# Attention mixers of a two-block kernel: head norms of the keys by tokens, the gates' remainders on another engine, three merge buffers, two weight loads placed anew

## The chip, the cores and the metric

The kernel runs on one core of one Trainium2 chip. The metric is the device time of one execution in microseconds (us). Engines are named PE (TensorE, matmuls), PEld (its weight loads), DVE (VectorE), ACT (ScalarE), POOL (GpSimd) and SP (SyncE, which here issues the DMAs).

## The reference, cut to what matters

The program is two transformer-like blocks in float32 on 256 tokens of width 1024. The first has two layers, each an FFN, a *mixer* and an FFN; then come an even mixer, an MLP, an odd mixer and an MLP. The change touches only the two mixers (stages m0 and m1) of the first block.

```python
h = rms_norm(x, mix_norm[l])
(nq, nkc, nvc, nks, nvs, nkw, nvw, ngate, sq, sk, sv, wq, wk, wv, bgate) = jnp.split(h @ w_in[l], ...)
y_nsa = nsa_attention(...)   # 8 query heads, 2 key heads: compressed, selected and window keys
y_sb = stick_breaking_attention(...)           # 4 heads, sq, sk, sv
y_swa = swa_sink_attention(...)                # 4 query heads, 2 key heads, wq, wk, wv
g = sigmoid(bgate).reshape(B, S, 3, 1024)
merged = g[:, :, 0] * (y_nsa @ w_up_nsa[l]) + g[:, :, 1] * (y_sb @ w_up_sb[l]) + g[:, :, 2] * (y_swa @ w_up_swa[l])
x = x + merged @ w_out[l]
```

Inside the attentions, queries and keys of each head (64 values) are normed: `rms_norm(q, q_norm)`, `rms_norm(k, k_norm)`. The compressed keys and values are `silu(blocks @ w1) @ w2`, the compressed key is normed too.

## The kernel before, in words

Activations lie with features on the 128 partitions and the 256 tokens along the free side. A float32 product is made of three matmuls on rounded halves (`product`, L675 to L677): the weights and the activations are split into a rounded part and a remainder. Every weight block is a **unit** of up to 128x2048 words, streamed through three raw buffers and three split buffers (AHEAD = 3). For a unit, SP loads the raw words, ACT copies the rounded part (`hi`, L1579, two halves), DVE or POOL subtracts to get the remainder (`lo`, DVE L2326, POOL L3302, two halves), and PE multiplies. A raw buffer is loaded again when the remainder of its unit is written (for kind "raw", when PE is done with it); a rounded part may be written when PE is done with the unit three places before. SP issues all loads in the order of the list made in `plan_mixer`. Each engine runs its own program in order; a call `hi(U[...] + 3)` stands where the engine prepares the unit three places further in the list.

A mixer runs, on PE: projections of the stick-breaking q, k, v; then queries and keys of the others, interleaved with `stick(0)` to `stick(5)` (stick-breaking attention) and `compress(kv, half)` (the w1 products, 32 matmuls of 30 columns each); `all_values` (values and head gates); then 24 *gates* (`gate(n)`, 24 matmuls of 256 columns each, for the 12 units "bg"), which are spread between the ten attention jobs of the list `jobs` (2 of kind "w", 8 of kind "n"): for job i, `second(i)` (transposes of P), `scores(i+1)`, `gate(4+2i)`, `third(i)` (times V), `gate(5+2i)`. Last are the three products "up" for each of 8 output blocks o, merged on DVE and POOL with the gates, and the product with w_out ("wo").

Head norms. For queries, `querysum` makes the mean squares with tokens on the partitions (8 numbers for a token), `querymean` copies them, and one root and one reciprocal with a Newton step (`exact`) serves all 24 columns; the factors are applied to the scores. For the keys "nk" (512 columns) and "wk" (256), `headsum` makes the means spread over all 128 partitions, `headroot` (ACT) takes the root, and `headnorm` (DVE: `exact`, five instructions on the whole width, L2603 to L2616, then a multiplication, L2629) scales the key. On PE, `third` waits for values, on DVE `first(x)` makes the biased scores and their maximum (L2536 or L2539, L2545), ACT the exponential (L1769), and `then(x)` the normed P (L2562 to L2573). `least` and `gated` do the same for the compressed keys; `compressed(1)` on PE transposes their result. PSUM banks go round in a ring of seven.

The remainders of the units three places after "bg" 1 to 11 are made by POOL, all others in the mixer by DVE. The merging uses two buffers `b.tm`.

The mark that PE awaits before the first "up" product:

```python
for x in new(at(s, "attended", "dve")):
    pe.wait_ge(*x)
```

Of the kernel before, what the change touches and what calls it, by code (L numbers as in the profile page):

```python
# [213 lines left out]
class Map:  # L214
# [158 lines left out]
    def lay_mixer(self):  # L373
# [15 lines left out]
        b.ms, b.rq = take(24), take(24)  # L389
# [17 lines left out]
        b.tm = [grid(take(768), c=3) for _ in range(2)]  # L407
# [145 lines left out]
    def plan_mixer(self, l):  # L553
# [29 lines left out]
        self.unit((s, "w2"), [(0, 128, kv * 128, 128, 2, 0, 64, t[f"nsa_cmp_{n}_w2"][l].rearrange("(k p) n -> p k n", p=128))  # L583
                              for kv, n in ((0, "k"), (1, "v"))], 256, "raw", 64)
        for blk in range(1, 12):
            gate(blk)
# [52 lines left out]
HN = {("q", 0): 0, ("q", 1): 1, "nk": 0, ("q", 2): 1, "wk": 0, "kc": 1}  # L639

# [10 lines left out]
def tensor_program(pe, L, M):  # L651
# [210 lines left out]
    def mixer(s, was, l):  # L862
# [27 lines left out]
        def querysum(name):  # L890
# [3 lines left out]
            for c in range(4):  # L894
                ins = pe.matmul(b[:, 2 * c:2 * c + 2], b_.hn[HN[name]][:, c * 128:c * 128 + 128], M.blk64[:, 0:128:64],
                                start=True, stop=True)
            ins.then_inc(*done((s, name, "ms"), (s, name, "hn")))

# [71 lines left out]
        querysum(("q", 0))  # L970
# [10 lines left out]
        querysum(("q", 1))  # L981
# [6 lines left out]
        headsum("nk", 512)  # L988
# [5 lines left out]
        querysum(("q", 2))  # L994
# [15 lines left out]
        headsum("wk", 256)  # L1010
        compress(1, 0)
        all_values(1)
        compress(1, 1)
# [9 lines left out]
        m = U[s, "w2"]  # L1023
        v2 = M.raw(m).rearrange("p (k n) -> p k n", k=4)
        b = bank(s, "kc")
        ready(m)
        for x in new(at(s, "hidT", 0, "s")):
# [10 lines left out]
        ins.then_inc(*done((s, "vc"), ("unit", m)))  # L1038
        gate(1)
# [527 lines left out]
def scalar_program(act, L, M):  # L1567
# [217 lines left out]
    def mixer(s, was, l):  # L1785
# [82 lines left out]
        headroot("nk", 512)  # L1868
# [8 lines left out]
        headroot("wk", 256)  # L1877
        for x in new(*[at(s, ("q", i), "msv") for i in range(3)]):
# [10 lines left out]
        hi(U[s, "va", 1] + 3)  # L1889
        hidden(1)  # L1890
        hi(U[s, "w1", 1, 1] + 3)
# [17 lines left out]

        gate(0)  # L1910
        headsq("kc", M.bank(s, "kc")[:, 0:15], 15, ("kc",))
        hi(U[s, "w2"] + 3)
# [4 lines left out]
        gate(1)  # L1917
# [20 lines left out]
        gate(2)  # L1938
        headroot("kc", 15)
        weights(0)  # L1940
# [23 lines left out]
        for blk in range(4):  # L1964
            for j in range(2):
# [5 lines left out]
                act.activation(b_.Mr[:, o, :], b_.tm[o % 2][:, 0, :], ACT.Copy, scale=1.0).then_inc(*done((s, "Mh", o)))  # L1971
# [316 lines left out]
def vector_program(dve, L, M):  # L2288
# [286 lines left out]
    def mixer(s, was, l):  # L2575
# [55 lines left out]
        def querymean(x_):  # L2631
            name = ("q", x_)
# [988 lines left out]
```

## Time and profile before

| | before |
|---|---|
| median of 3 runs | 2646.88 us (2639.64 to 2652.54) |
| the profiled execution, its own time | 2644.85 us |
| its span in the trace | 2642.9 us (1.95 us lie around it) |
| PE busy | 2514.2 us, 95% |
| DVE, ACT, POOL busy | 1628.0, 1189.7, 470.0 us |
| mean granted clock of PE | 0.970 of full speed |
| mixer m0 | about 240 to 503 us of the span |
| mixer m1 | about 940 to 1202 us |

The span is what the profiler saw from the first to the last instruction. A granted clock of 1.00 is 2.4 GHz, of 0.50 it is 1.2 GHz; PE has no other level here, and a number between is a mean over a stretch. A matmul counts as busy also where it runs at half the clock.

### The profile page before, as it was taken

Reading aid. Unit: us, or ns where it says so; the run is one execution under the profiler, and the core shown is the slowest. Engines: PE = TensorE matmul, PEld = TensorE weight load, DVE = VectorE, ACT = ScalarE, POOL = GpSimd, SP = SyncE. Lnnn points to the kernel's source line nnn. Section 1 sums busy time; section 2 is a strip of 40 time slices with the busy share of each in tenths; the row PEclk is TensorE's granted clock in tenths of the full one; section 3 lists DMA queues with packets and bytes.
Section 4 is the critical chain, followed back from the end, with each engine's and each line's share of the span. In section 5 each row is a group of like instructions: output and inputs, shape, how many; then the busy total and the mean of one; then the engine's idle time right before and its main releaser. Section 6 shows DMA issues by size and latency. Waiting matters only on the chain.

```text
span 2642.9 us, 42197 instructions
## 1 busy us (share of the span) xinstructions
PE 2514.2 (95%) x17977; PEld 2333.5 (88%) x17977; DVE 1628.0 (62%) x2410; ACT 1189.7 (45%) x1952; POOL 470.0 (18%) x429
## 2 busy tenths in 40 slices
PE   8999979999999898899999988999999999999998
PEld 7999879999999898799998764888888999999998
DVE  4777656677888865657776676553343654556753
ACT  5444446544444454455544444342232443444653
POOL 1321015432022100362423120200001011001000
PEclk8999879999999998899999998999999999999999
DMA  6667444476766755346777220132323333334563
GB/s 220 213 213 219 122 144 112 150 233 214 249 222 227 236 149 169 93 125 220 255 259 219 64 76 1 48 112 96 94 98 92 126 96 98 110 105 135 165 197 101
DMA packets 386384, 401.65 MB, mean 152 GB/s; under 512 B 44695, under 2 KB 370611, under 8 KB 385940
## 3 DMA queue, kind: packets, MB, share of 16 engines
q1 hardware_dynamic: 383448, 391.19, 47.3%
q10 hardware_dynamic: 2748, 7.76, 0.8%
q8 instruction: 141, 2.31, 0.4%
q14 instruction: 47, 0.39, 0.0%
HBM read 394.72 MB, written 4.19 MB: 151 GB/s over the span
## 4 chain that ended last, share of the span: by engine, by line
PE 73%; DVE 17%; ACT 6%; issue 2%; DMA 2%; POOL 1%; ACTq 0%; DVEq 0%; SPq 0%; POOLq 0%
PE bank L675 22%; PE bank L676 21%; PE bank L677 21%; DVE rounded L2326 5%; DVE plain L2315 3%; ACT rounded L1579 3%; PE bank L683 2%; PE bank L688 2%; PE bank L1515 1%; DVE plain L2573 1%; POOL plain L3366 1%; PE bank L1078 1%; DMA plain<-in_w_in 1%; PE bank L1108 0%; DVE plain L2562 0%
## 5 line engine op out<-in xcount | busy, mean ns | idle before, releaser
L675 PE MATMUL bank<-rounded 128*128 128x256 f32 (+1 forms) x3704 | 1126.2, 304 | 24.8 <-DVE rounded L2326 9.7
L676 PE MATMUL bank<-rounded 128*128 128x256 f32 (+1 forms) x3704 | 1107.3, 299 | 0.0
L677 PE MATMUL bank<-rounded 128*128 128x256 f32 (+1 forms) x3704 | 1106.3, 299 | 0.0
L2326 DVE TENSOR_TENSOR rounded<-plain,rounded 128x1024 fp32r<-128x1024 f32 (+2 forms) x574 | 671.3, 1216 | 486.5 <-ACT rounded L1579 486.2
L675 PEld LDWEIGHTS bank<-rounded 128*128 128x128 f32 x3704 | 721.8, 195 | 60.8 <-DVE rounded L2326 12.5
L1579 ACT ACTIVATE rounded<-plain 128x1024 fp32r<-128x1024 f32 (+1 forms) x630 | 616.9, 1032 | 341.5 <-PE bank L677 283.9
L676 PEld LDWEIGHTS bank<-rounded 128*128 128x128 f32 x3704 | 722.6, 195 | 16.6
L677 PEld LDWEIGHTS bank<-rounded 128*128 128x128 f32 x3704 | 722.0, 195 | 16.6
L675 PE MATMUL bank<-rounded,rounded 128*128 128x256 f32 (+2 forms) x1472 | 453.9, 308 | 24.0 <-DVE rounded L2326 18.4
L676 PE MATMUL bank<-rounded,rounded 128*128 128x256 f32 (+2 forms) x1472 | 451.1, 306 | 0.0
L677 PE MATMUL bank<-rounded,rounded 128*128 128x256 f32 (+2 forms) x1472 | 449.6, 305 | 0.0
L675 PEld LDWEIGHTS bank<-rounded,rounded 128*128 128x128 f32 x1472 | 280.4, 190 | 41.3 <-DVE rounded L2326 21.6
L676 PEld LDWEIGHTS bank<-rounded,rounded 128*128 128x128 f32 x1472 | 282.9, 192 | 12.4
L677 PEld LDWEIGHTS bank<-rounded,rounded 128*128 128x128 f32 x1472 | 281.5, 191 | 11.6
L3302 POOL TENSOR_TENSOR rounded<-plain,rounded 128x1024 fp32r<-128x1024 f32 x56 | 133.6, 2409 | 449.5 <-ACT rounded L1579 449.5
L2315 DVE SCALAR_TENSOR_TENSOR plain<-plain 128x1024 f32<-128x1024 f32 x140 | 189.8, 1402 | 1.4 <-DMA plain<-in_ada_w 0.8
L3366 POOL TENSOR_TENSOR plain<-plain 128x256 f32<-128x256 f32 x88 | 72.6, 832 | 402.7 <-ACT plain L1739 391.4
L1739 ACT ACTIVATE plain<-plain 128x256 f32<-128x256 f32 x88 | 36.9, 419 | 195.7 <-DVE plain L2501 195.7
L688 PE MATMUL bank<-plain 128*128 128x128 f32 (+2 forms) x475 | 73.6, 297 | 53.3 <-DVE plain L2573 20.5
L3319 POOL TENSOR_TENSOR plain<-plain 128x256 f32<-128x256 f32 (+1 forms) x64 | 58.4, 913 | 358.9 <-ACT plain L1633 356.8
L688 PEld LDWEIGHTS bank<-plain 128*128 128x128 f32 (+2 forms) x475 | 56.8, 147 | 65.2 <-DVE plain L2573 20.2
L683 PE MATMUL bank<-plain 128*128 128x30 f32 (+5 forms) x564 | 101.6, 337 | 2.2 <-POOL plain L3429 2.0
(302 smaller groups left out, 2090.7 us busy)
## 6 DMA issues: line engine op xcount, KB each, us to landing
plain<-in_mlp_w SPq DMA_DIRECT2D x64, 1024.0 KB, 5.3
plain<-in_ada_w SPq DMA_DIRECT2D x48, 1024.0 KB, 5.4
plain<-in_ffn_w_gate SPq DMA_DIRECT2D x44, 1024.0 KB, 5.5
plain<-in_ffn_w_up SPq DMA_DIRECT2D x44, 1024.0 KB, 5.9
plain<-in_ffn_w_down SPq DMA_DIRECT2D x32, 1024.0 KB, 5.2
plain<-in_w_in SPq DMA_DIRECT2D x32, 1024.0 KB, 5.3
plain<-in_od_w_in SPq DMA_DIRECT2D x32, 1024.0 KB, 5.7
plain<-in_ffn_w_down SPq DMA_DIRECT2D x16, 768.0 KB, 5.4
```

The lines of the kernel that those rows point to most:

```text
L675: pe.matmul(dst, a[0], b[0], start=first and i == 0, stop=False)
L676: pe.matmul(dst, a[0], b[1], start=False, stop=False)
L677: ins = pe.matmul(dst, a[1], b[0], start=False, stop=last and i == n - 1)
L683: ins = pe.matmul(dst, a, b, start=first and i == 0, stop=last and i == n - 1)
L688: ins = pe.transpose(o, i, ident[0:i.shape[0], 0:i.shape[0]])
L1579: act.activation(top, raw, ACT.Copy, scale=1.0).then_inc(*done(("hi", m, half)))
L1739: act.activation(f.sg[:, c % 4, :], f.sg[:, c % 4, :], ACT.Silu, bias=0.0, scale=1.0).then_inc(*done((s, "silu", c)))
L2315: dve.scalar_tensor_tensor(acc, raw[:, i, :], M.cc[:, k, v:v + 1], acc, MUL, ADD).then_inc(*done(*keys))
L2326: dve.tensor_tensor(low, raw, top, SUB).then_inc(*done(("lo", m, half)))
L3302: pool.tensor_tensor(low, raw, top, SUB).then_inc(*done(("lo", m, half)))
L3319: pool.tensor_tensor(acc, acc, sq[c % 2], ADD).then_inc(*done((s, "acc", c)))
L3366: pool.tensor_tensor(f.sg[:, c % 4, :], f.sg[:, c % 4, :], f.up[c % 4], MUL).then_inc(*done((s, "gu", c)))
```

## The change

1. Keys "nk" and "wk" get their mean squares by tokens too (`tokensum`, `tokenmean`), beside the queries: `b.ms` and `b.rq` grow from 24 to 36 columns, and one root and one `exact` serve all. As the keys need their factor along the free side and on all partitions of a head, PE then spreads it (`keyfactors`: 12 matmuls of 128 columns with a broadcast column as weights) into two banks, and DVE multiplies (`keyscale`).
2. All remainders of the gates' units go to DVE: three ahead of and beside the first job, one at the end of each job i (`lo(U[s, "bg", 2 + i] + 3)`). POOL has none left in a mixer.
3. Merging goes round in three buffers, and POOL makes the remainder of block o-1 after the sums of block o.
4. w2 is no unit any more: SP loads it into its own 256 words by two DMAs of 64 KB, beside the third unit after the first query block. The second half of w1 for the values stands behind gate unit 0 in the list, and `compress(1, 1)` behind `gate(0)` on PE. `hidden(1)` and the splits on ACT are placed to match.

```diff
@@ plan_mixer
         values(1)
-        w1(1, 1)
-        def gate(blk):
+        for blk in range(12):
+            if blk == 1:
+                w1(1, 1)
             self.square((s, "bg", blk), w, 0, 8, 2584 + blk * 256, 256)
-        gate(0)
-        self.unit((s, "w2"), [...], 256, "raw", 64)
-        for blk in range(1, 12):
-            gate(blk)
@@ tensor_program
+MS = {("q", 0): 0, ("q", 1): 8, ("q", 2): 16, "nk": 24, "wk": 32}
-        def querysum(name):
+        def tokensum(name, n=4):
...
+        def keyfactors():
+            for x in new(at(s, "rq")):
+                pe.wait_ge(*x)
+            for name, n in (("nk", 4), ("wk", 2)):
+                b = bank(s, name, "r")
+                for c in range(n):
+                    for g in range(2):
+                        f = MS[name] + 2 * c + g
+                        ins = pe.matmul(b[g * 64:g * 64 + 64, c * 128:c * 128 + 128], b_.rq[:, f:f + 1].to_broadcast([128, 64]),
+                                        ident, start=True, stop=True)
+                ins.then_inc(*done((s, name, "r")))
-        headsum("nk", 512)
+        tokensum("nk")
         stick(4)
...
         all_values(0)
-        headsum("wk", 256)
+        tokensum("wk", 2)
         compress(1, 0)
         all_values(1)
-        compress(1, 1)
...
         gate(0)
-        m = U[s, "w2"]
+        compress(1, 1)
+        keyfactors()
+        gate(1)
         (products "kc" and "vc" with w2)
-        gate(1)
@@ scalar_program
-        headroot("nk", 512)
         hi(U[s, "wq"] + 3)
...
         hi(U[s, "va", 0] + 3)
-        headroot("wk", 256)
-        for x in new(*[at(s, ("q", i), "msv") for i in range(3)]):
+        for x in new(*[at(s, name, "msv") for name in MS]):
             act.wait_ge(*x)
         act.activation(b_.rq, b_.ms, ACT.Sqrt, ...)
         hidden(0)
         hi(U[s, "w1", 1, 0] + 3)
-        hi(U[s, "va", 1] + 3)
-        hidden(1)
-        hi(U[s, "w1", 1, 1] + 3)
         (evictions of the values, the head gates)
+        hi(U[s, "va", 1] + 3)
         gate(0)
+        hidden(1)
+        gate(1)
         headsq("kc", ...)
-        hi(U[s, "w2"] + 3)
         (eviction of "vc")
-        gate(1)
         gate(2)
+        weights(0)
         headroot("kc", 15)
-        weights(0)
+        hi(U[s, "w1", 1, 1] + 3)
         gate(3)
@@ vector_program
+        def keyscale(name, dst, n):
+            for x in new(at(s, name, "r"), L.last()):
+                dve.wait_ge(*x)
+            dve.tensor_tensor(dst, dst, M.bank(s, name, "r")[:, 0:n], MUL).then_inc(*done((s, name, "s"), ("free", s, name, "r")))
         headscale(("q", 2), ...)
-        headnorm("nk", b_.nk, 512)
+        tokenmean("nk")
         lo(U[s, "wq"] + 3)
...
         stick(5)
+        tokenmean("wk", 4)
         lo(U[s, "va", 0] + 3)
-        headnorm("wk", b_.wk, 256)
-        exact((s, "rqroot"), b_.rq, b_.ms, b_.cst[:, 0:24])
+        exact((s, "rqroot"), b_.rq, b_.ms, b_.hnt[:, 0:36])
         lo(U[s, "w1", 1, 0] + 3)
         lo(U[s, "va", 1] + 3)
         hidden(1)
-        lo(U[s, "w1", 1, 1] + 3)
-        lo(U[s, "bg", 0] + 3)
+        keyscale("nk", b_.nk, 512)
+        keyscale("wk", b_.wk, 256)
         headscale("kc", ...)
-        lo(U[s, "w2"] + 3)
         first(0)
+        lo(U[s, "bg", 0] + 3)
+        then(0)
         headnorm("kc", b_.kc[:, 0:15], 15)
-        then(0)
+        lo(U[s, "w1", 1, 1] + 3)
+        lo(U[s, "bg", 1] + 3)
         for i in range(n):
             (first(i + 1), then(i + 1), least or gated, keep of job i)
+            lo(U[s, "bg", 2 + i] + 3)
         here(s, "attended", "dve")
-                b, b2, tm = M.bank(s, "up", o), M.bank(s, "up2", o), b_.tm[o % 2]
-                for x in new(..., at(s, "M", o - 2) if o >= 2 else None):
+                b, b2, tm = M.bank(s, "up", o), M.bank(s, "up2", o), b_.tm[o % 3]
+                for x in new(..., at(s, "M", o - 3) if o >= 3 else None):
@@ gpsimd_program
-        for blk in range(1, 12):
-            lo(U[s, "bg", blk] + 3)
         for o in range(6):
             (two sums of block o)
-            (remainder of block o)
+            if o:
+                merged_rest(o - 1)
+        merged_rest(5)
@@ sync_program
+                if h == 2:
+                    for kv, name in enumerate(("nsa_cmp_k_w2", "nsa_cmp_v_w2")):
+                        sp.dma_start(grid(M.mix.w2[:, 128 * kv:128 * kv + 128], k=2), ...)
```

In the new order the units are ..., va 0, w1(1,0), va 1, bg 0, w1(1,1), bg 1, bg 2, ..., bg 11, wu 0 to 3, wo 0 to 3. So three places after va 0 stands bg 0, after va 1 bg 1, after bg 0 bg 2, after w1(1,1) bg 3, after bg k (k from 1) bg k+3, and after bg 11 it is wu 2.

## Rows read from the trace of the kernel before

**Rows 1.** Stretches of the mixers: busy by engine, PE's clock, DMA share, GB/s.

```profile
311.05:390.89 79.84, 58.90 (x401) 55.06 (x401) 45.37 (x107) 35.23 (x77) 9.38 (x4) 0.78 0.48 148
1010.26:1089.91 79.65, 60.03 (x401) 56.14 (x401) 43.96 (x105) 35.27 (x77) 9.38 (x4) 0.76 0.46 141
390.89:463.85 72.96, 72.96 (x632) 65.15 (x632) 41.01 (x92) 43.77 (x115) 36.84 (x16) 0.98 0.38 109
463.85:499.86 36.01, 32.73 (x267) 31.95 (x265) 20.09 (x38) 20.30 (x25) 21.62 (x21) 1.00 0.36 118
```

The columns of busy time are PE, PEld, DVE, ACT and POOL, each with its count of instructions.

**Rows 2.** Waits of PE in 240 to 500 us: total, times, longest.

```profile
PE bank L926 <- DVE plain L2712: 5.1, 1, 5.1
PE bank L688 <- DVE plain L2573: 4.4, 1, 4.4
PE bank L688 <- DVE plain L2562: 4.0, 1, 4.0
PE bank L688 <- DVE plain L2790: 3.7, 1, 3.7
PE bank L675 <- ACT plain L1898: 2.6, 1, 2.6
PE bank L675 <- DVE plain L2844: 1.4, 2, 1.1
PE bank L675 <- DVE rounded L2326: 1.3, 1, 1.3
```

**Rows 3.** Stretches, PE alone: width, busy, clock, DMA share, GB/s.

```profile
337.43:342.88 5.45, 5.45 (x26) 0.50 0.97 299
378.47:381.62 3.15, 3.15 (x28) 1.00 0.00 0
303.66:307.32 3.66, 3.66 (x35) 1.00 0.00 0
```

**Rows 4.** DVE in order of time around the norm of "nk": start, length.

```profile
303.89 3.35 DVE L2603 RECIPROCAL plain<-plain 128x512 f32<-128x512 f32 x1 [1.25 <-ACT plain L1808]
...
309.93 0.69 DVE L2629 TENSOR_TENSOR plain<-plain 128x512 f32<-128x512 f32 x1
310.54 1.92 DVE L2326 TENSOR_TENSOR rounded<-plain,rounded 128x816 fp32r<-128x816 f32 x2
```

**Rows 5.** ACT in order of time, 328 to 357 us.

```profile
333.76 2.00 ACT L1579 ACTIVATE rounded<-plain 128x1024 fp32r<-128x1024 f32 x2 [6.55 <-DMA plain<-in_w_in]
...
355.12 1.28 ACT L1808 ACT_TABLE_LOAD   x1
356.42 0.28 ACT L1808 ACTIVATE plain<-bank,plain 128x15 f32<-128x15 f32 x1
```

**Rows 6.** DVE, then POOL, in order of time, 361 to 368 us.

```profile
361.83 0.48 DVE L2573 TENSOR_SCALAR plain<-plain 128x128 f32<-128x128 f32 x2
...
362.62 4.52 DVE L2573 TENSOR_SCALAR plain<-plain 128x128 f32<-128x128 f32 x2
...
362.42 4.65 POOL L3302 TENSOR_TENSOR rounded<-plain,rounded 128x1024 fp32r<-128x1024 f32 x2 [109.09 <-ACT rounded L1579]
```

**Rows 7.** One job in the later jobs: DVE, then ACT, then PE.

```profile
416.43 0.75 DVE L2536 SCALAR_TENSOR_TENSOR plain<-bank,plain 128x512 f32<-128x512 f32 x1 [2.71 <-PE bank L1078]
...
419.58 1.50 DVE L2569 TENSOR_TENSOR plain<-plain 128x2 f32<-128x2 f32 x1
...
422.24 0.62 DVE L2573 TENSOR_SCALAR plain<-plain 128x256 f32<-128x256 f32 x2
...
415.19 1.99 ACT L1579 ACTIVATE rounded<-plain 128x1024 fp32r<-128x1024 f32 x2
...
423.31 1.04 PE L688 MATMUL bank<-plain 128*128 128x128 f32 x8
```

**Rows 8.** ACT in order of time, 466 to 472 us, where the gates end.

```profile
467.03 0.39 ACT L1905 ACTIVATE plain<-bank 128x256 f32<-128x256 f32 x1 [2.78 <-PE bank L677]
467.31 2.00 ACT L1579 ACTIVATE rounded<-plain 128x1024 fp32r<-128x1024 f32 x2
```

More of the change, by code:

```diff
@@ L388, in lay_mixer @@
         b.kc = take(16)
-        b.ms, b.rq = take(24), take(24)
+        b.ms, b.rq = take(36), take(36)
+        b.w2 = take(256)
         b.vc = grid(take(128), c=2)
@@ L406, in lay_mixer @@
         b.Mf, b.Mr, b.Ml = (grid(a, c=8) for a in self.take_split(2048))
-        b.tm = [grid(take(768), c=3) for _ in range(2)]
+        b.tm = [grid(take(768), c=3) for _ in range(3)]
         b.jobs = [("w", 0, i) for i in range(2)] + [("n", j, i) for j in range(4) for i in range(2)]
@@ L969, in mixer @@
         query(1)
-        querysum(("q", 0))
+        tokensum(("q", 0))
         b = bank(s, "ncs")
@@ L980, in mixer @@
         project(m, (0, 1), b).then_inc(*done((s, "nk"), ("unit", m)))
-        querysum(("q", 1))
+        tokensum(("q", 1))
         stick(2)
@@ L993, in mixer @@
         project(m, (0,), b).then_inc(*done((s, "wk"), ("unit", m)))
-        querysum(("q", 2))
+        tokensum(("q", 2))
         stick(5)
@@ L1022, in mixer @@
         gate(0)
-        m = U[s, "w2"]
-        v2 = M.raw(m).rearrange("p (k n) -> p k n", k=4)
+        compress(1, 1)
+        keyfactors()
+        gate(1)
+        v2 = grid(b_.w2, k=4)
         b = bank(s, "kc")
-        ready(m)
-        for x in new(at(s, "hidT", 0, "s")):
+        for x in new(at(s, "w2"), at(s, "hidT", 0, "s")):
             pe.wait_ge(*x)
@@ L2717, in mixer @@
         query(1)
-        querymean(0)
+        tokenmean(("q", 0))
         windows(0)
@@ L2839, in mixer @@
                 o = 2 * blk + j
-                b, b2, tm = M.bank(s, "up", o), M.bank(s, "up2", o), b_.tm[o % 2]
-                for x in new(at(s, "up", o), at(s, "sig", blk), at(s, "M", o - 2) if o >= 2 else None):
+                b, b2, tm = M.bank(s, "up", o), M.bank(s, "up2", o), b_.tm[o % 3]
+                for x in new(at(s, "up", o), at(s, "sig", blk), at(s, "M", o - 3) if o >= 3 else None):
                     dve.wait_ge(*x)
@@ L3398, in mixer, with merged_rest @@
                 *done(("h", s, c)))
-        for blk in range(1, 12):
-            lo(U[s, "bg", blk] + 3)
+        def merged_rest(o):
+            for x in new(at(s, "Mh", o)):
+                pool.wait_ge(*x)
+            pool.tensor_tensor(b_.Ml[:, o, :], b_.tm[o % 3][:, 0, :], b_.Mf[:, o, :], SUB).then_inc(*done((s, "M", o)))
         for x in new(at(s, "attended", "pe"), at(s, "attended", "act"), at(s, "attended", "dve"), L.last()):
@@ L3532, in sync_program @@
                     sp.wait_ge(*x)
+                if h == 2:
+                    for kv, name in enumerate(("nsa_cmp_k_w2", "nsa_cmp_v_w2")):
+                        sp.dma_start(grid(M.mix.w2[:, 128 * kv:128 * kv + 128], k=2),
+                                     t[name][l].rearrange("(k p) n -> p k n", p=128)).then_inc(*M.land("compress").done((s, "w2")))
                 n = 384 if h < 8 else 256
```

22 lines of the change are left out of this document (8 added, 14 removed).

## The prediction

> **What bounds the kernel now.** I read the table of busy times first: PE is busy 95% of the span, so nearly all the change can win is PE's idle time and its slow clock in the two mixers. The stretches of the mixers [rows 1] show where that is. From the end of the projection of "wk" and its sum (311.05 us) to the first transpose of the compressed P (390.89 us), PE is busy 58.9 of 79.84 us and its clock is 0.78; m1 has the same stretch with 79.65 us and 0.76. From there to the last gates (72.96 us) PE never waits, and in the merging (36.01 us) it stands idle 3.3 us. So three stretches must be looked at one by one: a bad one of 79.8 us, in which 20.9 us are idle, a full one, and a nearly full one. The waits of PE [rows 2] name the idle times: 5.1 us for `stick(5)`, 4.0 and 4.4 us for the P of the first job, 3.7 us for the compressed P, 2.6 us for the head gates' bank, and in the merging 1.4 us for the tm products and 1.3 us for a remainder of wo. A gate of 24 matmuls takes 5.45 us at 1.2 GHz and 3.15 us at 2.4 GHz [rows 3]; the slow one follows the small matmuls of a compress and a short wait. That is a second cost of each wait.
>
> **The sum.** I follow PE through m0, from 311.05 us, in the order of the new program.
>
> *Norms.* Before, DVE works on the norm of "nk" from 303.89 to 310.62, then on a remainder to 312.46, and only then on `stick(4)`, for which `stick(5)` on PE waits 5.1 us [rows 2, 4]. Now it copies 8 columns, well under half a microsecond; the remainder ends near 305, the weights of `stick(4)` near 308.7, and PE comes to `stick(5)` at 311.0. The wait goes wholly: 5.1 us. Behind it the values start at 312.6 instead of 317.6, and need no slow clock from this idle time. The price is on PE: 12 matmuls of 128 columns. No row has them; below they cost nothing (as cover in a wait), above twelve times 0.12 us at full clock and twice that at half. I take 1.0 us, near the 0.13 us that one of the eight transposes takes [rows 7]; the range is 0 to 3 us. `keyscale` is one instruction of 0.69 us like L2629 [rows 4] and a half one for "wk", on DVE, beside the gate matmuls of `gate(1)`. `tokensum` is 8 matmuls of 2 columns instead of one of 512; I take the two as equal.
>
> *Loads.* Before, bg 0 is loaded only after `compress(1, 0)`, and ACT waits for it 6.55 us, until 333.76 [rows 5]; its remainder is ready at 337.3, and `gate(0)` starts then at half clock. Now bg 0's raw buffer is that of va 0, free near 305, so it follows va 1 on SP's queue near 313 and lands near 319; ACT and DVE have it at 322.7. PE runs values 0, the sum of "wk", compress(1, 0), values 1 and is at `gate(0)` near 327: covered by 4 us. w1(1,1) and bg 1 are issued when compress(1, 0) ends (321.5) and, two blocks of 1 MB at the 299 GB/s of [rows 3] plus some 2 us, land near 327 and 330; compress(1, 1) is reached at 330: covered by 3 us. w2's two DMAs of 64 KB take SP about a microsecond in a place where nothing waits for loads; I price it at nothing. Were that cover gone, it would be 1 us for each mixer. The 2.6 us for the head gates' bank go, since their sigmoid (until 328.7) now runs under `gate(0)`.
>
> *The first job.* Doing the same for each step, PE is at scores(0) near 341 (before 351.0), at `second(0)` near 347.3. DVE makes first(0), the remainder of bg 2 (2.36 us) and then(0): P is ready at 348.0 and 348.9. The wait is 1.2 us instead of 4.0. The second wait of 4.4 us is of another kind: DVE's L2573 takes 4.52 us where the same instructions just before take 0.48, and ends with POOL's two remainders, which run 4.65 us beside it [rows 6]. POOL has no remainders left in the mixer, so this wait goes. The exponentials of job 0 now come ahead of the root of "kc", which costs ACT one table load of 1.28 us behind them; compressed(0) is not held up by more than what the matmuls before it take.
>
> Here a page bears on it. In the rows, ACT loads a table at 355.12 for 1.28 us, and the root starts at 356.42, 0.02 us later, with no drain between them [rows 5]. The Trainium skill (ScalarE: Activation LUTs, What ACT_TABLE_LOAD costs) states that each switch costs a drain of about 1.38 us besides, 2.66 us in all. By that rule the chain of "kc", which has two switches from the exponentials to compressed(0)'s key and on to job 1, would be an estimated 2.8 us longer in each mixer, and the sum 5.6 us smaller; the trace does not agree.
>
> *New waits.* The remainders of bg 3 and bg 4 (2 x 2.36) stand ahead of first(1) on DVE, so P of job 1 is ready at 361.0, just as PE gets there. Then `least` frees the banks of scores(2) at 362.8 (0.8 us of waiting). ACT holds `gate(5)`'s eviction and the split of bg 5 behind the exponential of the compressed scores, and so the copies for third(1) are late by 1.5 us. The remainder of bg 5 delays first(2), and gated ends at 374.3 where PE is ready at 369.2: 5.1 us instead of 3.7. Total waits: 1.2 + 0.8 + 1.5 + 5.1 = 8.6 us, against 20.9.
>
> *The bad stretch.* PE's own work at full clock, by the lengths of [rows 3] for gates (8 of them, 3.14 each) and compresses (2, 3.65 each), 9.5 us for the two values blocks, and small ones, is 50.9 us with the 1.0 us of keyfactors. Before it is 49.9, so that 58.9 - 49.9 = 9.0 us went to the slow clock. I let half of it stand (4.5 us): the idle gaps ahead of values 0 and gate 0 go, the compresses and the small matmuls around the first job stay and the clock fell behind such stretches before too. New length: 50.9 + 4.5 + 8.6 = 64.0 us. That is 15.8 us less than 79.8; m1 has the same waits and instructions, 79.65, so 15.6 less.
>
> *Later jobs.* PE needs 8.6 to 9.1 us for a job. Each remainder on DVE now waits for ACT's split, which waits for the job's second gate. In the job shown, ACT splits from 415.19 to 417.18 [rows 7]; DVE would subtract until 418.6, and first(x), which began at 416.43, begins 2.1 us later. But its chain is 6.4 us long (416.43 to 422.86) only because L2569 takes 1.50 us next to POOL; without, 5.1. So P is whole at 423.7; PE reads its first half at 423.31 and the second half 0.5 us later, at 423.8. It just fits: 0 for each job.
>
> *Merging.* The mark "attended" of DVE now stands behind the remainder of wu 2, which waits for the split that ACT runs from 467.31 to 469.31 [rows 8]. So PE, which before went straight from gate(23) (466.9) to the products "up", waits until 470.8: a new wait of 3.9 us. ACT's sigmoids, which began at 470.62, hardly move. But the waits of 1.4 and 1.3 us later on go, as three buffers and the lagged remainder let POOL and DVE follow PE's 2.93 us per block, and they are most of the 3.3 us idle [rows 1, 2]. Net +0.6 at most, +0.3 taken for each mixer.
>
> In all -15.8 - 15.6 + 0.6 = -30.8 us. On the profiled execution's 2644.85 us this gives 2614.0. The median of three is 2.0 us above that execution, within their spread of 13 us, so I leave 2614.
>
> **The rivals.**
>
> *A: half of it is given back.* All waits shrink, but the clock stays as slow as before (9.0 us instead of 4.5) and each of the chained queues on ACT and DVE holds PE a further 4 us. For it: the clock here falls behind small matmuls, which keyfactors adds to. Against: the idle gaps that preceded two of four slow stretches go. Saving 2 x 7.3 = 14.6 us: 2630.
>
> *B: slower, DVE's order sets the jobs.* The remainder stands between `keep` and the next first(x), and waits for a split that waits for PE. If first(x) starts 2.1 us later and the chain does not get shorter by the 1.3 us, or ACT's splits come later, PE waits in each job by what the chain lacks; a closed loop of PE, ACT and DVE carries it from job to job. At 2 us in each of 10 jobs and two mixers it is 40 us, with the 3.9 us twice 48, against 31.4 won: 2661. It decides from 1.6 us for a job on. For it: only 0.1 us of room in the job worked out. Against: DVE is busy 41.0 of 72.96 us there, and 8 x 2.4 more leave 13 us.
>
> *C: the stretch is bound by loads anyway.* Before, ACT waits for a load ahead of bg 0 [rows 5]. If bg 0 and bg 1 land 6 to 8 us later than I work out, then only the POOL contention (4.4) and little else is won: 2640. Against: the DMA share in the stretch is 0.48 [rows 1].
>
> *D: the clock hardly falls any more and the new waits don't come.* Then the saving is 2 x (15.8 + 4.5 + 3) = 47: 2598.
>
> **How the numbers follow.** My forecast has 0.6, A 0.2, D 0.06, C 0.09, B 0.05. From no change (2646.9) a measurement of this kernel tells about 0.5%, 13.2 us, so faster means below 2633.6. That holds for the forecast, A (mostly) and D: 0.84; C is the same, with a part of A: 0.11; B is slower: 0.05. The range leaves out B and most of C, and has the bounds of keyfactors (2 us for each mixer up, 1 down) and of the clock (4.5 us each way) within it: 2597 to 2634.
>
> **What would show it.** The wait for `stick(5)` gone; ACT's split of bg 0 near 320; scores(0) 9 to 10 us earlier; no DVE L2573 group above 1 us beside a remainder; the stretch from the wk sum to the compressed transposes near 64 us; a new wait of 3.9 us for a DVE remainder ahead of "up" in each mixer; no wait in the later jobs; the waits in the merging gone. The prediction is wrong if PE waits for P in the later jobs, or for w1(1,1) or bg 1, or if the clock in the stretch stays below 0.8.

## The result, and the profile after

The changed kernel takes 2608.28 us, the median of 4 runs (2605.64 to 2609.9), beside 2646.2 us for the kernel before on the same chip. The ratio is 0.9856, with a 95% interval of 0.983 to 0.9882. The forecast was 2614.0 us, faster, with a range of 2597 to 2634.

The table of busy times of the changed kernel, to be read beside the one before:

```profile
PE 2497.8 (96%) x18041; PEld 2319.9 (89%) x18041; DVE 1629.0 (63%) x2438; ACT 1190.7 (46%) x1950; POOL 367.0 (14%) x385
```

PE has 64 matmul records more and is busy 16.4 us less (before 2514.2), because more of its work runs at full clock. Only 13.5 us of that lie in the three stretches of the mixers that are compared below; another 5.4 lie ahead of the first mixer, in code that both kernels share, and other stages give some back. POOL has lost 103 us of remainders. The span is 2603.8 us instead of 2642.9, that is 39.1 less.

Where they come from is seen in the stretches. The rows are width, then busy time of PE, PEld, DVE, ACT, POOL, PE's clock, the DMA share and GB/s. First the bad stretch of m0 and of m1 after the change, in the bounds of [rows 1]:

```profile
305.95:367.70 61.75, 53.52 (x427) 50.43 (x426) 37.89 (x100) 35.91 (x75) 0.00 (x0) 0.90 0.64 197
988.72:1047.30 58.58, 50.36 (x428) 47.39 (x427) 37.80 (x100) 35.98 (x75) 0.00 (x0) 0.95 0.65 200
```

They were 79.84 and 79.65 us [rows 1], so they have lost 39.2 us together. Of the 18.1 us that m0's stretch lost, 12.7 are idle time of PE (20.94 before, 61.75 - 53.52 = 8.23 after) and 5.4 are busy time. Then the later jobs, and the time from the last gates to the next FFN (all of the merging and of wo), after and before:

```profile
367.70:441.15 73.45, 73.45 (x633) 65.48 (x633) 48.64 (x108) 44.02 (x115) 0.00 (x0) 0.97 0.37 102
441.15:502.89 61.74, 57.83 (x456) 57.54 (x457) 40.11 (x65) 33.73 (x49) 21.19 (x25) 0.94 0.46 148
```

```profile
390.89:463.92 73.03, 73.03 (x633) 65.22 (x633) 41.01 (x92) 43.77 (x115) 36.91 (x16) 0.98 0.38 109
463.92:524.59 60.67, 57.39 (x458) 56.61 (x457) 38.94 (x65) 33.64 (x49) 26.40 (x28) 0.97 0.49 157
```

The jobs stay as they were, with PE busy throughout. The end of the mixer is 1.1 us longer (in m1 0.9). With 0.8 us more in the jobs of both mixers, the mixers give 36.3 of the 39.1 us. The other 2.8 lie in code that both kernels share. The stretches up to the start of m0 are 240.58 us before and 235.45 after, 5.1 us apart with the same instructions (PE is busy 225.63 and 220.28 us of them), and other stages give a part of it back. I take it for chance between two executions: in e12, which is the changed kernel once more, the mixer m0 starts at 239.84 us. So times within m0 are compared from the start of the bad stretch, not from the start of the span.

The waits of PE in m0 after (total, times, longest), which answer to [rows 2]:

```profile
PE bank L685 <- DVE plain L2799: 4.5, 1, 4.5
PE bank L672 <- DVE rounded L2332: 3.9, 1, 3.9
PE bank L1120 <- ACT plain L1791: 1.3, 1, 1.3
PE bank L685 <- DVE plain L2568: 0.9, 1, 0.9
PE bank L1087 <- DVE plain L2772: 0.8, 1, 0.8
PE bank L1060 <- DVE plain L2635: 0.4, 1, 0.4
PE bank L685 <- DVE plain L2579: 0.4, 1, 0.4
```

The waits for `stick(5)` (5.1), for the head gates (2.6), and the two of 4.0 and 4.4 for the first job are gone or under 1 us. The one for the compressed P, which `gated` makes (L2799), has grown from 3.7 to 4.5. The second row is new: PE stands at the mark "attended" until DVE has made the remainder of wu 2, although the first "up" products use wu 0.

### The profile page after: what moved, and what is told of

The parts are those of the page before. It is cut to its first block, busy times and chain, and to the rows that moved or that the text cites. A ratio compares the mean times of both kernels' runs of the same rounds, so it can differ in the third digit from the quotient of the medians.

```text
span 2603.8 us, 42299 instructions
## 1 busy us (share of the span) xinstructions
PE 2497.8 (96%) x18041; PEld 2319.9 (89%) x18041; DVE 1629.0 (63%) x2438; ACT 1190.7 (46%) x1950; POOL 367.0 (14%) x385
## 4 chain that ended last, share of the span: by engine, by line
PE 74%; DVE 17%; ACT 5%; issue 2%; DMA 1%; POOL 1%; ACTq 0%; DVEq 0%; SPq 0%
PE bank L672 22%; PE bank L673 21%; PE bank L674 21%; DVE rounded L2332 6%; PE bank L680 3%; DVE plain L2321 3%; ACT rounded L1588 2%; PE bank L685 2%; PE bank L1524 1%; DVE plain L2579 1%; POOL plain L3379 1%; ACT plain L1778 1%; PE bank L1087 1%; PE bank L1117 0%; DVE plain L2456 0%
## 5 line engine op out<-in xcount | busy, mean ns | idle before, releaser
L2332 DVE TENSOR_TENSOR rounded<-plain,rounded 128x1024 fp32r<-128x1024 f32 (+1 forms) x618 | 722.6, 1216 | 518.9 <-ACT rounded L1588 518.7
L673 PEld LDWEIGHTS bank<-rounded 128*128 128x128 f32 x3704 | 717.5, 194 | 16.4
L685 PE MATMUL bank<-plain 128*128 128x128 f32 (+2 forms) x475 | 74.2, 298 | 41.0 <-DVE plain L2579 12.7
L685 PEld LDWEIGHTS bank<-plain 128*128 128x128 f32 (+2 forms) x475 | 57.1, 148 | 53.1 <-DVE plain L2579 20.1
L680 PEld LDWEIGHTS bank<-plain 128*128 128x128 f32 (+2 forms) x564 | 80.3, 193 | 20.2 <-issue 12.3
```

The lines of the kernel that those rows point to most:

```text
L673: pe.matmul(dst, a[0], b[1], start=False, stop=False)
L680: ins = pe.matmul(dst, a, b, start=first and i == 0, stop=last and i == n - 1)
L685: ins = pe.transpose(o, i, ident[0:i.shape[0], 0:i.shape[0]])
L2332: dve.tensor_tensor(low, raw, top, SUB).then_inc(*done(("lo", m, half)))
```

## The experiments

Each was timed beside the kernel before on the same chip, whose medians were 2642.63 (e1 to e4), 2644.75 (e5 to e8) and 2646.2 us (e9 to e12), so across sets the ratios are compared. The interval of a ratio is some 0.002 each way, or 5 to 6 us: a difference of 5 us between two ratios is inside it, and rests on the rows of both mixers. These too vary with the same program: the bad stretches of the changed kernel take 61.75 and 58.58 us in one profile and 60.33 and 60.12 in the other (e12). "The mixers" below means m0 and m1 from their start to the next FFN (last column but one of the table in the next section). L numbers shift by a few lines between kernels. The first experiments ask which of the four parts brings the gain.

**e1: POOL makes the gates' remainders again.** The changed kernel with part 2 undone.

```diff
         lo(U[s, "w1", 1, 1] + 3)
-        lo(U[s, "bg", 1] + 3)
...
-            lo(U[s, "bg", 2 + i] + 3)
         here(s, "attended", "dve")
 (pool_program)
+        for blk in range(1, 12):
+            lo(U[s, "bg", blk] + 3)
```

> The changed kernel with the remainders of the units three places after bg 1 to 11 back on POOL; all else as changed. By the prediction's steps, DVE's P of a job is held up beside POOL's remainders (4.4 us of waiting in the first job before), while the wait of 3.9 us for the mark ahead of the products up goes: the two about cancel, 2608 us within 4, and a wait of 2 to 4 us for P of job 1 shows in each mixer. Rival: POOL's remainders did harm only where the first job's P stood right behind the split of its unit in the old order, and now they stand beside nothing that PE waits for; then only the 3.9 us for each mixer and about 1 us of delayed P go: 2598 us.

Measured: 2600.17 us, 0.9838 (0.9816 to 0.9859), near the rival's 2598: by the ratios some 5 us faster than the changed kernel (the mixers are 5.3 us shorter, and 6.3 against e12). The stretches and waits of m0:

```profile
305.64:366.83 61.19, 51.01 (x427) 47.38 (x426) 37.60 (x96) 35.77 (x75) 9.71 (x4) 0.95 0.63 190
366.83:440.43 73.60, 73.60 (x633) 65.81 (x633) 41.01 (x92) 43.71 (x115) 36.88 (x16) 0.97 0.39 108
440.43:498.11 57.68, 55.66 (x457) 55.06 (x457) 36.53 (x63) 33.50 (x49) 26.01 (x28) 1.00 0.50 159
```

```profile
PE bank L685 <- DVE plain L2799: 4.7, 1, 4.7
PE bank L685 <- DVE plain L2579: 1.9, 3, 1.1
PE bank L672 <- DVE rounded L2332: 1.5, 2, 1.3
```

With POOL's remainders back, the wait of 4.4 us for the first job's P does not come back (the second row is three waits of 1.1 and less). The wait of 3.9 us at the mark is gone, and the end of the mixer takes 57.68 instead of 61.74 us. So within the changed kernel the move to DVE is no part of the gain; by these rows it costs. Of POOL's contention about half a microsecond is left: PE waits 1.1 us for the first half of P of job 1, where in e12 (the changed kernel once more) it waits 0.6.

**e2: part 2 alone on the kernel before.** The same lines, the other way round, in the kernel before.

> The kernel before with this one part of the change: all remainders of the gates' units on DVE. By the prediction's steps the wait of 4.4 us for P of job 0 goes in each mixer, a wait of 3.9 us ahead of up comes, and the transposes of the compressed P wait 0.8 us more: within 2 us of before, with the three rows as named. Rival: freeing DVE from POOL is worth more than its one wait, since the clock stays up too behind a shorter wait: 2636 us, 5 us faster for each mixer.

Measured: 2636.06 us, 0.9977 (0.9965 to 0.999), so some 6 us: the rival's number. The bad stretches take 75.51 and 73.25 us, 10.7 less than before; the ends of the mixers take 1.8 more. Its waits in m0:

```profile
PE bank L675 <- ACT plain L1898: 5.6, 1, 5.6
PE bank L675 <- DVE rounded L2326: 4.4, 2, 3.9
PE bank L688 <- DVE plain L2562: 4.0, 1, 4.0
...
PE bank L688 <- DVE plain L2573: 0.4, 1, 0.4
```

Here the 4.4 us for L2573 do go, as the prediction said, and the mark costs 3.9 us. The 5.6 us for the bank of the head gates (2.6 before) are no price of this edit: in m1 they are 4.4 and 4.2. Nor is the clock the gain, as the rival had it: of the 10.7 us, 9.6 are idle time of PE (20.94 and 19.62 us before, 16.97 and 13.98 now) and 1.1 busy time.

**e3: the norms of the keys undone.** Part 1 out of the changed kernel: `headsum`, `headroot` and `headnorm` for "nk" and "wk" again, no `keyfactors`, no `keyscale`.

```diff
-        tokensum("nk")
+        headsum("nk", 512)
...
-        keyfactors()
...
-        tokenmean("nk")
+        headnorm("nk", b_.nk, 512)
```

> The changed kernel with the norms of nk and wk as before (sum on 128 partitions, one chain of five wide instructions for each, no 12 matmuls on PE). By the prediction's steps the wait for stick(5) of 3.6 to 5.1 us comes back, with a slow clock for the values behind it (some 2 us), less 1.5 us for the 12 matmuls that go: 5 us more for each mixer, 2618 us. Rival: the later part of the stretch is set by loads and by ACT's and DVE's queues, which take up most of a delay at its start: 1 to 2 us for each mixer, 2611 us.

Measured: 2618.9 us, 0.9908 (0.9886 to 0.993), as expected: some 12 us slower than the changed kernel (the mixers are 11.5 us longer). Its bad stretch in m0, and the wait for `stick(5)`, which is back with its old length:

```profile
313.36:379.67 66.31, 54.43 (x400) 50.99 (x401) 44.21 (x111) 37.63 (x79) 0.00 (x0) 0.86 0.59 183
```

```profile
PE bank L936 <- DVE plain L2723: 5.1, 1, 5.1
```

**e9: the norms alone on the kernel before.**

> The kernel before with the norms of nk and wk by tokens (the 12 matmuls behind the first gate), all else as before. Undone in the changed kernel this part cost 5 to 6 us for each mixer. Theory: it is worth the same alone, the wait of 5.1 and 3.6 us for stick(5) less 1.5 us, and a faster clock behind it: 10 us in all, 2635 us. Rival: in the old order the waits behind it (for the bank of the head gates, for P of job 0) take up what it wins: under 2 us for each mixer, 2642 us.

Measured: 2642.57 us, 0.998 (0.9967 to 0.9994), the rival's number. The 5.1 us for `stick(5)` are gone, and yet the bad stretch of m0 has shrunk by 1.5 us only, and that of m1 has grown by 0.5 (80.18); the rows of m0 say why:

```profile
313.43:391.75 78.32, 60.24 (x426) 56.53 (x426) 39.11 (x96) 33.57 (x73) 9.37 (x4) 0.80 0.50 150
```

```profile
PE bank L685 <- ACT plain L1912: 5.3, 1, 5.3
PE bank L690 <- DVE plain L2587: 4.4, 1, 4.4
```

```profile
338.20 2.00 ACT L1595 ACTIVATE rounded<-plain 128x1024 fp32r<-128x1024 f32 x2 [4.50 <-DMA plain<-in_w_in]
342.65 1.59 PE L685 MATMUL bank<-plain 128*64 128x15 f32 x16 [5.34 <-ACT plain L1912]
```

PE comes to `gate(0)` at 332.73 us, 4.7 earlier than before, runs it and the 12 new matmuls, and then stands ahead of the products with w2: 5.3 us for the bank that ACT's sigmoid of the head gates frees (L1912), where it was 2.6. In the old order that sigmoid stands on ACT behind the split of bg 1, and ACT waits 4.50 us for that unit's load (4.11 before). So a load was awaited in the old order, and PE felt it through the head gates.

**e10: the order alone on the kernel before.** Part 4 and the splits placed to match; the norms, POOL's remainders and the two buffers as before.

> The kernel before with the order alone changed: w2 in its own words, w1(1,1) behind gate unit 0, and the queues of ACT and DVE around the first job as in the changed kernel (splits, hidden(1), weights(0) ahead of the root of kc, then(0) ahead of its norm, the remainders of bg 2 and bg 3 behind first(0)); norms, POOL's remainders and two buffers as before. Theory: the single undone parts add up to far less than the whole gain since the order is most of it: the waits of 2.6 to 4.2 us for the bank of the head gates, of 4.0 and of 4.4 us for P of job 0 all go in this kernel, though POOL still has its remainders: 10 us or more for each mixer, 2622 us. Rival: the order is worth what its undone list entry cost, 1 to 2 us for each mixer, and the 4.4 us beside POOL stay: 2641 us.

Measured: 2618.77 us, 0.9893 (0.9871 to 0.9915), as the theory had it. The bad stretches of m0 and m1, and the first waits of m0:

```profile
313.95:380.90 66.95, 54.44 (x400) 50.99 (x401) 43.95 (x107) 37.55 (x79) 9.66 (x4) 0.86 0.57 174
...
1001.87:1067.19 65.32, 54.34 (x401) 50.97 (x401) 42.49 (x105) 37.54 (x79) 9.66 (x4) 0.86 0.56 169
```

```profile
PE bank L936 <- DVE plain L2723: 5.1, 1, 5.1
PE bank L685 <- DVE plain L2798: 4.7, 1, 4.7
```

The order alone takes 27.2 us out of the two stretches, where the whole change takes 39.2; 17.1 of the 27.2 are idle time and 10.1 busy time. The waits of 2.6, 4.0 and 4.4 us all go with it (0.9 and 0.4 stay), although POOL still makes the remainders. Why the last goes is in DVE's order of time, then POOL's:

```profile
354.48 0.48 DVE L2580 TENSOR_SCALAR plain<-plain 128x128 f32<-128x128 f32 x2
...
355.27 0.48 DVE L2580 TENSOR_SCALAR plain<-plain 128x128 f32<-128x128 f32 x2
...
359.48 4.98 POOL L3312 TENSOR_TENSOR rounded<-plain,rounded 128x1024 fp32r<-128x1024 f32 x2 [103.30 <-ACT rounded L1587]
```

Before, the second half of `then(0)` and POOL's first pair of remainders began within 0.2 us of each other (362.62 and 362.42, [rows 6]). In the new order P is finished at 355.8, and POOL starts 3.7 us later. They no longer meet. In e1 it is the same: P at 341.65, POOL from 345.37.

**e4: only w1(1,1) back in front of bg 0.** Part 4 halved: w2 stays out of the units, `compress(1, 1)` stands ahead of `gate(0)` again, and the split of w1(1,1) comes earlier to match.

```diff
         values(1)
+        w1(1, 1)
         for blk in range(12):
-            if blk == 1:
-                w1(1, 1)
```

> The changed kernel with the second half of w1 for the values ahead of gate unit 0 again, in the list and on PE, with ACT's and DVE's splits in the order of the list; w2 stays in its own words. By the prediction's steps the place of bg 0 in the list removed a wait for its load: a wait of some 2 us ahead of the first gate and a slow clock behind it come back, 3 us or more for each mixer, 2615 us. Rival: with the rest of the change, PE reaches the first gate only 10 us after the raw buffer is free, and load, split and remainder take 8 to 9: no wait, 2608 us.

Measured: 2611.89 us, 0.9881 (0.986 to 0.9902), between the two expectations: by 3 us in the mixers and some 6 by the ratios slower than the changed kernel, at the edge of what can be told. The bad stretches take 61.82 and 60.64 us:

```profile
308.78:370.60 61.82, 56.31 (x427) 53.21 (x427) 37.72 (x100) 36.22 (x75) 0.00 (x0) 0.86 0.62 189
...
993.21:1053.85 60.64, 54.74 (x427) 51.56 (x427) 37.56 (x99) 36.12 (x75) 0.00 (x0) 0.89 0.61 186
```

No wait of PE comes ahead of `gate(0)`, although ACT waits 3.92 us for the load of bg 0 and splits it only at 324.81. PE is idle less than in the changed kernel (5.51 us against 8.23 in m0) and busy for longer (56.31 against 53.52). So of part 4 it is not the place of w1(1,1) that carries the gain. What e4 keeps and e10 has too is w2 off the units, and the new places of ACT's and DVE's splits with it; the two were not tried apart.

**e5: two merging buffers in the changed kernel**, and the remainder of block o at once (`b_.tm[o % 2]`, `merged_rest(o)`).

> The changed kernel with merging in two buffers and POOL's remainder of a block right after its sums, as before; all else as changed. By the prediction's steps the waits of 1.4, 0.6 and 1.3 us in the merging come back, 3 us or so for each mixer: the part from the last gate to the sums of the next stage 64 to 65 us instead of 61.7, 2614 us in all. Rival: behind the wait of 3.9 us for the mark, DVE and POOL are no longer late against PE, so two buffers do: 61.7 us, no change, 2608 us.

Measured: 2610.5 us, 0.9876 (0.9853 to 0.9899): not told apart from the changed kernel. The ends of the mixers take 62.48 and 62.07 us against 61.74 and 61.58, and PE is idle there for 4.37 and 4.35 us against 3.91 and 3.90. Behind the wait at the mark the third buffer wins half a microsecond for each mixer, and no more. Without that wait it wins more: the end of the mixer takes 57.68 us in e1 with three and 59.13 in e10 with two.

The others ask what the forecast's two remaining waits cost.

**e6: the remainder of wu 2 behind the mark.**

```diff
-            lo(U[s, "bg", 2 + i] + 3)
+            if i < n - 1:
+                lo(U[s, "bg", 2 + i] + 3)
         here(s, "attended", "dve")
+        lo(U[s, "bg", 11] + 3)
```

> The changed kernel with the last remainder (of wu 2) made by DVE behind its mark attended instead of ahead of it. By the prediction's reading the wait of 3.9 us ahead of up goes in each mixer and nothing takes its place, as DVE is idle until the sigmoids are there: 57.7 us from the last gate on, 7.8 us less in all, 2600 us. Rival: DVE makes the first merging products later, and POOL and the banks make PE wait for most of it: 2606 us.

Measured: 2602.59 us, 0.9844 (0.9822 to 0.9866), between the two and nearer the first. The end of the mixer is the same in m0 and m1 (57.68):

```profile
444.10:501.78 57.68, 55.65 (x457) 55.06 (x457) 38.91 (x65) 33.49 (x49) 20.19 (x25) 1.00 0.49 161
```

By the ratios this is 3 to 5 us faster than the changed kernel (the mixers 4.7). The 3.9 us are gone, and so is the slower clock that came with them (0.94 before this edit, 1.00 now: 57.83 us busy in m0 against 55.65). Small waits of 1.3, 0.5 and 0.3 us stand in their place.

**e7: e6, and `gated` one job earlier.** `gated()` stands behind `keep` of job 0 on DVE, ahead of the remainder of bg 5, instead of behind `first(2)` and `then(2)`.

```diff
-            elif i == 1:
-                gated()
             kind, j, t = b_.jobs[i]
...
+            if i == 0:
+                gated()
```

> As the run before this one, and gated (the norm of the compressed P) made at the end of job 0 on DVE, ahead of the remainder and of first(2), instead of behind then(2). Theory: the wait of 4.5 us for the compressed P goes, and the clock stays up behind it: 5 to 6 us less for each mixer, 2590 us. Rival: P of job 2 comes 1.6 us later and the wait moves there: 2 us less for each mixer, 2596 us.

Measured: 2588.06 us, 0.9785 (0.9765 to 0.9805), 14.5 us faster than e6. The three stretches of m0, then the bad one of m1:

```profile
309.39:364.99 55.60, 51.86 (x426) 48.88 (x426) 34.56 (x88) 33.72 (x65) 0.00 (x0) 0.94 0.62 191
364.99:436.46 71.47, 71.47 (x635) 64.28 (x633) 51.92 (x120) 45.70 (x125) 0.00 (x0) 1.00 0.42 119
436.46:494.13 57.67, 55.65 (x457) 55.06 (x457) 38.91 (x65) 33.51 (x49) 20.19 (x25) 1.00 0.49 160
...
979.68:1033.72 54.04, 50.29 (x427) 47.38 (x427) 34.47 (x88) 33.72 (x65) 0.00 (x0) 0.97 0.64 198
```

The wait for L2799 is gone, and behind it the jobs need 71.47 us at a clock of 1.00, where the kernels with that wait need 72.8 to 74.2. Against e6 the bad stretch of m0 lost 6.1 us and the jobs 2.1 (in m1 6.1 and 1.8): by these rows a wait of 4.5 us was worth 8 for each mixer, by the medians 7.

**e8: e1 and the earlier `gated`, POOL still making the remainders.**

> The first experiment's kernel (remainders of the units three places after bg 1 to 11 on POOL) with gated at the end of job 0. Theory: the same 5 to 6 us less for each mixer as with the remainders on DVE, 2589 us, with P of job 2 untouched since no remainder stands on DVE. Rival: POOL's remainder of bg 5 now runs beside gated and first(2) and DVE is held up by 2 us or more: 2595 us.

Measured: 2599.62 us, 0.9821 (0.9798 to 0.9845), slower than both expectations and 11.6 us slower than e7. The wait for `gated` shrinks to 1.9 us only. POOL, then DVE, in order of time:

```profile
366.97 4.67 POOL L3313 TENSOR_TENSOR rounded<-plain,rounded 128x1024 fp32r<-128x1024 f32 x2 [8.65 <-ACT rounded L1588]
```

```profile
366.98 2.39 DVE L2796 TENSOR_SCALAR plain<-plain 128x8 f32<-128x8 f32 x1
369.40 2.50 DVE L2799 TENSOR_TENSOR plain<-plain 128x240 f32<-128x240 f32 x1
```

In the changed kernel these two instructions take 0.23 and 0.41 us. Here each is held by one of POOL's two. This is what the move to DVE is good for, once `gated` stands where POOL would meet it.

**e11: e7, and ACT's split of bg 5 behind the copies for `third(1)`**, so that they don't wait behind it.

> The kernel with the mark ahead of the last remainder and gated at the end of job 0, and besides ACT's split of bg 5 moved behind the copies of job 1's transposes, for which third(1) waits 1.2 us. Theory: that wait goes, 1.2 us for each mixer, 2585 us. Rival: the remainder of bg 5 and first(2) come 1 us later on DVE and P of job 2 becomes late: no gain, 2588 us.

Measured: 2586.84 us, 0.9772 (0.975 to 0.9794). The wait of 1.2 us for those copies is gone, but waits of 0.6 and 1.7 us on DVE (L2544, L2581) take its place. From e7 it can't be told.

**e12: the changed kernel once more.**

> The changed kernel itself beside the others, on the same chip: 0.9856 of before as in its first timing, 2607 us, by every theory.

Measured: 2609.52 us, 0.9861 (0.9835 to 0.9887). Its bad stretches are 60.33 and 60.12 us, together 120.45; in the first profile they were 120.33.

## Why the prediction was right

The waits of PE that would go, stay and come were foreseen nearly one by one, and they carry the result. One cause was wrong (why the 4.4 us go), one was wrong in the merging, and the work and the slow clock of the bad stretch were mis-sized.

The sums of both mixers, in us, from such rows. The end of a mixer is from the last gates to the next FFN; "mixers in all" counts from their start, so it holds some 140 us more.

| kernel | bad stretch | later jobs | end of the mixer | mixers in all | ratio |
|---|---|---|---|---|---|
| before | 159.5 | 146.2 | 121.3 | 566.4 | 1 |
| e9, norms alone | 158.5 | 146.2 | 119.8 | 565.5 | 0.998 |
| e2, remainders on DVE alone | 148.8 | 146.1 | 123.1 | 559.0 | 0.9977 |
| e10, order alone | 132.3 | 147.8 | 118.3 | 539.3 | 0.9893 |
| e1, and norms and three buffers | 122.0 | 146.4 | 115.4 | 524.8 | 0.9838 |
| after, and remainders on DVE | 120.3 | 146.9 | 123.3 | 530.1 | 0.9856 |
| e12, the same kernel again | 120.4 | 147.4 | 122.1 | 531.1 | 0.9861 |
| e7, both waits taken out | 109.6 | 143.1 | 115.3 | 509.2 | 0.9785 |

**Norms.** Right. The wait for `stick(5)` goes wholly, and comes back with 5.1 us in e3. The price on PE was taken as 1.0 us (range 0 to 3) and is 1.53:

```profile
329.37 1.53 PE L905 MATMUL bank<-plain 128*64 128x128 f32 x24
```

The 12 matmuls leave 24 records. What the prediction did not say is that this gain hangs on the order: alone it is worth 1 us of the stretches (e9), which can't be told from nothing, behind the new order 10 (e10 to e1, where the third buffer comes too, but works only at the end of the mixer).

**Loads.** Right in what it says of PE: it waits for no load in that place, and e10 shows this part as the greatest, 27 us. e4 shows that the place of w1(1,1) has little share in it. That no load came late also answers case C; its 2640 us don't follow from its own terms, for two waits of 4.4 us off 2644.85 leave 2636. ACT waits 0.92 us for bg 0 and has it before PE asks for it:

```profile
315.50 2.00 ACT L1588 ACTIVATE rounded<-plain 128x1024 fp32r<-128x1024 f32 x2 [0.92 <-DMA plain<-in_w_in]
```

That is 9.6 us after the start of the bad stretch (305.95), where the same split of [rows 5] came 22.7 us after it (333.76 against 311.05). The text put it "near 320", 9 us after. The scores of job 0 start 28.8 us after that start; they were forecast at 30 and came at 40 before.

**The first job: here a step was wrong, though its size stood.** "POOL has no remainders left in the mixer, so this wait goes": the 4.4 us go, but in the new order they would have gone without that. In e10 and e1 POOL has all its remainders and the wait is gone, because P is finished before POOL starts. The contention itself was read rightly: e2 takes it away alone, loses the 4.4 us for L2573, and shortens the two stretches by 10.7 us. But the two cures don't add up. The prediction counted 8.8 us for a part that earns 1.7 in the stretches once the order is changed (e1 to after), and loses 7 to 8 at the end of the mixer. That the sum came out near is luck in this term: the order would have brought the 8.8 us by itself.

Of this contention the Trainium skill (SBUF — State Buffer, Who interferes with whom) says that DVE and GpSimd share one pair of ports, which the first to start holds for a whole instruction. The rows of e8 agree: 2.39 and 2.50 us on DVE beside 4.67 us for POOL's two instructions, about 2.3 each; and so does the 4.52 us beside 4.65 of [rows 6], again two beside two.

**The table load.** Right for P of the first job: the root of "kc" takes nothing from it. The key that this root makes comes 0.4 us late for PE (the row for L2635 above). ACT's rows after, its two loads and what follows each:

```profile
339.00 1.28 ACT L1778 ACT_TABLE_LOAD   x1
340.30 0.40 ACT L1778 ACTIVATE plain<-plain 128x128 f32<-128x128 f32 x1
...
342.15 1.28 ACT L1817 ACT_TABLE_LOAD   x1
343.45 0.28 ACT L1817 ACTIVATE plain<-bank,plain 128x15 f32<-128x15 f32 x1
```

The next instruction starts 0.02 us after the end of each load. The drain of about 1.38 us that the Trainium skill states (ScalarE: Activation LUTs, What ACT_TABLE_LOAD costs) is not there after the change either.

**New waits.** Predicted 8.6 us in the stretch, measured 8.2. They were 5.1 for the compressed P (4.5), 1.5 for `third(1)` (1.3), 1.2 for the first P (0.9) and 0.8 for `least` (0.8); two of 0.4 us (L2635, L2579) were not foreseen.

**Work and slow clock: mis-sized.** The prediction put 50.9 us of work at full clock and 4.5 us of slow clock in each mixer, 55.4 us busy. Measured are 53.52 and 50.36 us, and 51.01 and 51.92 in e12, 51.7 in the mean. Both terms were too large. An estimate from the two rows of e7, which have the same matmuls: m0 is busy 51.86 us with a clock of 0.94 over 55.60 us, m1 50.29 with 0.97 over 54.04. That is some 6.7 and 3.2 us at the lower level, so 3.5 us of it cost 1.6 us of busy time, and some 48.8 us of work at full clock are left. By that the work was taken 2.1 us too large, and the slow clock costs 1.6 to 4.7 us, 2.9 in the mean, instead of 4.5. One reason for the first is in the rows: a gate was counted with its whole length of 3.14 us, but the next group starts before the last matmul has ended, 2.98 us after the gate's start:

```profile
352.25 0.38 PE L672 MATMUL bank<-rounded 128*128 128x256 f32 x1
...
355.23 1.03 PE L685 MATMUL bank<-plain 128*128 128x128 f32 x8
```

For eight gates this makes 1.3 us. The same holds before: less the 1.5 us of the 12 matmuls some 47.3 us were work, so by this estimate the slow clock cost some 12 us in each mixer there, not 9.0, and the change gave back three quarters of it, not half. With the waits the bad stretches are 61.75, 58.58, 60.33 and 60.12 us instead of 64.0. It is the greatest error of the sum: 7.7 us for both mixers (128.0 against 120.3), part of the way to the case called D in the clock, while D's other half, no new waits, did not come. Case A, the clock as slow as before, is refuted: 0.90 and 0.95 instead of 0.78 and 0.76.

**Later jobs.** "It just fits" held, and case B is refuted. PE is busy in all of the 73.45 us although DVE makes eight more remainders there. DVE is busy 48.64 us instead of 41.01: eight remainders of 2.36 are 18.9, so some 11 us in which POOL had held DVE are gone. The chain of DVE is shorter, as said, for L2575 takes 0.16 us where it took 1.50 beside POOL:

```profile
381.33 0.16 DVE L2575 TENSOR_TENSOR plain<-plain 128x2 f32<-128x2 f32 x1
```

**Merging.** The wait at the mark was forecast at 3.9 us and is 3.9. All other waits there are gone, so PE is idle 3.91 us instead of 3.28 in the end of m0: 0.6 more, the prediction's "at most". But it took 0.3, and the end is 1.1 and 0.9 us longer. The other 0.4 (0.3 in m1) are busy time, behind the new wait: the clock is 0.94 over the end of the mixer where it was 0.97, and 1.00 in e6 without the wait. The reason given for the waits that go was wrong, though: it is not the three buffers. In e5, with two, all but 0.5 us of them is gone as well; I take it that PE, having stood at the mark, comes to these products late enough for DVE and POOL. What three buffers gain without that wait (e10 to e1, 2.9 us for both) is less than the wait costs.

In all: 39.2 us won in the bad stretches against 31.4 forecast, 0.8 lost in the jobs against 0, 2.0 lost in the end against 0.6, and 2.8 by chance elsewhere. The move of the remainders to DVE earns nothing in the changed kernel: e1, without it, is faster by the rows of both mixers, and the ratios agree though their intervals overlap.

What stays open: which of w2's place and the places of the splits carries the 27 us, and why the stretch of m0 had a slower clock in the first profile (53.52 us busy, 8.23 idle) than in e12 (51.01 and 9.32), with the same program. In e12 PE is faster and waits more: 1.5 us in three waits for P (L2579) instead of 0.4.

## What to carry to other kernels

Where a wait vanishes in a sum, ask which parts of the change would remove it each by itself; two that would, as here the order and the move off POOL, are worth one. The other way round, a part can be worth nothing until another is there, as the norms here: 1 us alone, 10 behind the new order. Price a wait of PE by what it does to the granted clock behind it too: here one of 3.9 us was worth 4 in the rows (other small waits took its place, but the clock rose), and one of 4.5 was worth 7 to 8. Before a piece of work is moved to the engine whose mark or result PE awaits, put the mark ahead of it: that (e6) was worth 3 to 5 us by the ratios, and `gated` earlier 14 more.

## What the runs showed of the hardware

- A remainder on POOL holds some DVE instructions for as long as it runs, however small they are: a DVE instruction of 8 columns takes 2.39 us beside it and 0.23 without (e8 and after). Not all kinds are held. In e1 POOL works from 359.06 to 363.74 us; beside it a TENSOR_REDUCE and a RECIPROCAL on DVE took 0.42 and 0.17 us, and the TENSOR_TENSOR of 2 columns behind them 1.86, until POOL had ended:

```profile
359.06 4.68 POOL L3313 TENSOR_TENSOR rounded<-plain,rounded 128x1024 fp32r<-128x1024 f32 x2 [8.66 <-ACT rounded L1588]
359.49 0.42 DVE L2551 TENSOR_REDUCE plain<-plain 128x2 f32<-128x256 f32 x1
361.89 1.86 DVE L2575 TENSOR_TENSOR plain<-plain 128x2 f32<-128x2 f32 x1
```

- PE's clock over 73 us of unbroken work depended on what lay just ahead of it. Behind the wait of 4.5 us the stretch had 0.97, behind one of 1.9 us (e8) 0.98, without the wait (e7) 1.00; from the first to the last it is a difference of 2 us.
- The stretch with most slow clock was shortened by work set earlier on the other engines: PE is busy 58.90 us at 0.78 before, 54.44 at 0.86 in e10 with one matmul record less, and 51.01 at 0.95 in e1 with 26 more.
